# A paged key/value cache loaded as rows of 8 KB, four tokens to a partition, and a bias product that reads its row in that order

## What is computed

```python
PAST_LEN = 4096; PAGE_SIZE = 128; DEC_BATCH = 8; DEC_SEQ = 8; N_HEADS = 8; HEAD_DIM = 64
# cache_k, cache_v (1, 320, 128, 8, 64) float32; page_table (8, 32)
def fox_attend(q, c_q, q_pos, k, v, c_k, k_pos):
    s = jnp.einsum('bqhd,bkhd->bhqk', q, k) * ATTN_SCALE
    bias = jnp.transpose(c_q, (0, 2, 1))[:, :, :, None] - jnp.transpose(c_k, (0, 2, 1))[:, :, None, :]
    s = jnp.where(causal[None, None], s + bias, -jnp.inf)
    p = jax.nn.softmax(s, axis=-1)
    return jnp.einsum('bhqk,bkhd->bqhd', p, v)

def one_seq(args):                       # for each of the 8 sequences
    pages, q_b, k_b, v_b, lf_b = args
    k_all = jnp.concatenate([cache_k[layer, pages].reshape(past, N_KV_HEADS, HEAD_DIM), k_b])
    v_all = jnp.concatenate([cache_v[layer, pages].reshape(past, N_KV_HEADS, HEAD_DIM), v_b])
    c = jnp.cumsum(lf_all, axis=0)
```

## Time and profile before

| | |
|---|---|
| median of 3 runs | 1596.27 us |
| lowest and highest of them | 1588.37 and 1600.27 us |
| span of the profiled execution, first to last instruction | 1590.7 us |
| PE busy | 1400.5 us, 88% of the span |
| DVE busy | 650.0 us |
| ACT busy | 387.5 us |
| mean rate of the DMAs | 267 GB/s |
| mean granted TensorE clock | 0.942 |

### The profile page before, as it was taken

How to read it: one execution, slowest core, us unless ns; L and a number is a source line. 1 busy time by engine, 2 the same in 40 slices (tenths; PEclk the granted TensorE clock), 3 DMA queues, 4 the chain that set the end, 5 groups by cost and what they waited for, 6 DMA issues and landing times. The chain is left out here.

```text
span 1590.7 us, 30783 instructions
## 1 busy us (share of the span) xinstructions
PE 1400.5 (88%) x10030; PEld 745.5 (47%) x10031; DVE 650.0 (41%) x1883; ACT 387.5 (24%) x1026; POOL 249.7 (16%) x291
## 2 busy tenths in 40 slices
PE   6999799999999999699888777777999989999992
PEld 3445566666667776344543322222333333444441
DVE  1423267776586666244543212212222322333333
ACT  1212264444444344311100111111111111111110
POOL 1000200004363220000011111111111111112120
PEclk9999799999999899989899889888999999999996
DMA  8312599999989799660073999999999999975836
GB/s 299 63 27 63 194 308 296 318 304 303 308 266 306 261 319 344 204 237 27 20 291 142 373 374 391 372 372 380 369 368 354 364 371 358 351 235 186 270 82 195
DMA packets 159803, 424.09 MB, mean 267 GB/s; under 512 B 48113, under 2 KB 50194, under 8 KB 133522
## 3 DMA queue, kind: packets, MB, share of 16 engines
q1 hardware_dynamic: 142912, 381.59, 66.5%
q0 software_dynamic: 14688, 38.83, 10.1%
q10 hardware_dynamic: 2098, 2.35, 0.5%
HBM read 395.25 MB, written 42.11 MB: 275 GB/s over the span
## 5 line engine op out<-in xcount | busy, mean ns | idle before, releaser
L2433 PE MATMUL ps_gu<-ring,mixT 128*32 128x512 f32 (+2 forms) x1664 | 368.2, 640 | 69.2 <-SPq L2223 68.3
L2433 PEld LDWEIGHTS ps_gu<-ring,mixT 128*32 128x32 f32 (+2 forms) x1664 | 126.4, 142 | 306.8 <-issue 269.7
L2450 PE MATMUL ps_y<-w_dn,aT_e 128*32 128x512 f32 (+2 forms) x832 | 175.9, 598 | 4.7 <-DVE aT_e L2367 2.5
L1427 PE MATMUL ps_kT<-ident,ring 128*128 128x128 f32 x1024 | 143.2, 282 | 16.5 <-DVE ring L1093 8.9
L1427 PEld LDWEIGHTS ps_kT<-ident,ring 128*128 128x128 f32 x1024 | 115.3, 145 | 74.8 <-issue 45.9
L2365 DVE TENSOR_TENSOR act_in<-sil,ps_gu 128x256 f32<-128x256 f32 x48 | 20.2, 421 | 302.0 <-ACT sil L2305 302.0
L2258 POOL DMA_INDIRECT kT<-h_dram,idx x50 | 51.8, 1037 | 454.5 <-DVE idx L2337 453.9
L2305 ACT ACTIVATE sil<-ps_gu 128x256 f32<-128x256 f32 x48 | 18.4, 383 | 403.9 <-PE ps_gu L2433 403.9
L1093 DVE COPY ring<-ps_kT 128x512 f32<-128x512 f32 x128 | 87.8, 686 | 42.2 <-PE ps_kT L1427 41.2
L2262 POOL DMA_INDIRECT sums_dram<-qT,sidx x50 | 79.9, 1599 | 149.7 <-DVE qT L2372 138.2
L2450 PEld LDWEIGHTS ps_y<-w_dn,aT_e 128*32 128x32 f32 (+2 forms) x832 | 55.4, 132 | 92.5 <-issue 84.2
(11 more groups left out here) (506 smaller groups left out, 1803.0 us busy)
## 6 DMA issues: line engine op xcount, KB each, us to landing
ring<-in_cache_k SPq DMA_DIRECT2D x256, 256.0 KB
ring<-in_cache_v SPq DMA_DIRECT2D x256, 256.0 KB, 4.5
ring<-in_w_gate_e SPq DMA_DIRECT2D x64, 1024.0 KB
ring<-in_w_up_e SPq DMA_DIRECT2D x64, 1024.0 KB
w_dn<-in_w_down_e SPq DMA_DIRECT2D x64, 1024.0 KB
w_in<-in_w_in SPq DMA_DIRECT2D x8, 1028.0 KB, 17.4
sums_dram<-w_dn SPq DMA_DIRECT2D x1, 4608.0 KB, 19.7
ring<-in_w_out SPq DMA_DIRECT2D x1, 4096.0 KB, 13.1
```

The costliest lines, as they stand in the source:

```text
L1427: last = pe.transpose(ps_kT[:, j % 2, e * PAGE:(e + 1) * PAGE], k_places[n % RING][:, e * DA + j * P:e * DA + (j + 1) * P], m.ident[:, :])
L2433: last = pe.matmul(ps_gu[at, :].rearrange("p (g n) -> p g n", g=2), xgT[:, u, k, at], w_gu[:, place, :, k, :].rearrange("p s g n -> p (s g ...
L2450: last = pe.matmul(ps_y[at, n, :], aT[:, j, at], w_dn[:, place, j, n * 512:(n + 1) * 512].rearrange("p s n -> p (s n)"), start=(j == 0), s ...
```

## The change

Each page is loaded into 32 partitions instead of 128: page i of the group goes to partitions i, i+4, i+8 and so on, and each partition takes four tokens that follow each other, one row of 8 KB. So column tile f of a place holds, in partition 4 k + i, token 4 k + f of page i. Keys and values are loaded in the same way, so scores and values agree. The bias row lies in the order of the tokens as before; the product that brings it in now names its 512 columns in the order (f, k, i), whose steps in the bias row are 1, 4 and 128 elements of 2 bytes, with i innermost. The order in which results are written is 0 to 511, as before. No instruction is added, removed or moved on any engine; the DMAs of L740 carry 32 rows of 2048 floats instead of 128 rows of 512.

```diff
@@ pages
             for i in range(GRP):
-                sp.dma_start(place[:, i * DA:(i + 1) * DA], cache[0, bass.ds(ids[i], 1)].rearrange("n k h d -> (n k) (h d)")).then_inc(arrived, 16)
+                sp.dma_start(place[i:P:GRP, :], cache[0, bass.ds(ids[i], 1)].rearrange("n (k f) h d -> (n k) (f h d)", f=FOLD)).then_inc(arrived, 16)
@@ past_scores
-                    pe.matmul(ps_sc[:, :], part_of[:, :, :, :].rearrange("a j e q -> a (j e q)"), bias[:, (n // 2) % 2, (n % 2) * COLS:(n % 2 + 1) * COLS],
-                              start=True, stop=False, skip_group_check=True)
+                    tokens = bias[:, (n // 2) % 2, (n % 2) * COLS:(n % 2 + 1) * COLS].rearrange("a (i k f) -> a f k i", i=GRP, f=FOLD)
+                    pe.matmul(ps_sc[:, :].rearrange("p (f k i) -> p f k i", f=FOLD, i=GRP), part_of[:, :, :, :].rearrange("a j e q -> a (j e q)"),
+                              tokens, start=True, stop=False, skip_group_check=True)
```

## The result

The changed kernel takes 1637.83 us (median of 4 runs, 1629.27 to 1649.23) where the kernel before, run beside it, takes 1598.27 us: a ratio of 1.0256, 95% interval 1.0213 to 1.0298. It is slower by two and a half per cent. The direction of the likeliest case was right; the time is 14 us above the upper end of the range (1590 to 1624 us), and only 0.32 had been given to a kernel slower by more than one per cent. All ratios here compare executions in the usual state of the chip; one of the five executions of e1_again, 6038.76 us, lies outside it and its cause is open. The profiled execution of after has a span of 1632.5 us, 41.8 more than the 1590.7 of before.

What follows compares the result with a forecast made beforehand. The prediction took PE to bound the stage, hiding the page loads. Dearer bias products added 11.1 us (13.4 less 2.3 absorbed), the stores' stall gave back 1.5: + 9.6 us, 1606 us, range 1590 to 1624.

Steps and rivals of the forecast that it cites:

- likeliest case: Whole kernel: 9.6 us slower, about 0.6%, at 1606 us; chance 0.56.
- the loads' gain: Page loads: 0.6 us less DMA time a turn, 38 us over 64 turns, hidden by PE.
- Value taken: 0.21 us, from the rows of the load itself: Bias product: each takes 0.21 us longer, priced from strided against contiguous weight loads; 64 products make 13.4 us.
- upper end: Bias product: 0.52 us longer each, from paces of strided and contiguous transposes; 33 us in all.
- 11 absorbed turns: Turns where PE waits anyway, ten for DVE's copy and one for the store; 2.3 us of added time absorbed there.
- rival 1: Bias product: strided read costs two or more access times a column, 0.52 us each; kernel 26 us slower, 1622 us; chance 0.23.
- both "ends": Bias product's price bounds: 0.01 us each, 1 us in all, and 0.52 us each, 33 us in all.
- part 1: Page loads: larger rows gain 1.5 us at the stores to `y_scr`, nothing elsewhere; bounds nothing and 7.2 us.
- that excess: SP's four page issues ahead of the `y_scr` stores took 0.94 us more than the next four; expected gone.
- the stall: PE stands 5.49 us near 641 us, as ACT waits for SP's stores to `y_scr`; expected about 4 us.
- slack of 4 us: Page loads: pages lie ready at least 4 us before use, so landing up to that much later costs nothing.
- Rival 3: Page loads: writes meet at fewer memory entries, under 286 GB/s; at 250 GB/s 70 us slower, 1665 us; chance 0.05.

Runs made afterwards that it cites:

- e1_again: Second run of the kernel before with only the bias product's reading order changed and the old page loads; ratio 1.0228 (1.0179 to 1.0276).
- experiment 5: Kernel before with its old loads, the bias product reading its row in eight different orders by turns; only each order's product time counted, 385 to 1071 ns.
- experiment 2: Kernel before with only the page loads changed to 8 KB rows on every fourth partition, old reading order; 1598.35 us, ratio 1.0016.
- experiments 7 to 9: Changed kernel's 8 KB rows on 32 neighbouring partitions (two bias reading orders), or every second partition of one half, old order: 1760.35, 1730.42, 1744.37 us.

## Why the prediction was wrong

Right was the frame. PE bounds the stage, it had nothing to do with the loads, the bias product is on PE's path, and its extra time reaches the turn in full but for some waits. The distance to L1443 moved by 0.65 us as the duration did, and the absorbed part was there (5.6 us of 41.1 as measured, about 10 by the table above, of which the rows name 4.7). That the loads' gain "is hidden by PE in all turns and is worth nothing there" held: the loads alone measured 1.0016.

**The step that failed** is the price of one product. The text has "Value taken: 0.21 us, from the rows of the load itself", and an "upper end" of 0.52 us. Measured is 0.652 us. With that value the same sum is 64 x 0.652 = 41.7 us, less 11 absorbed turns (7.2), less 1.5: + 33 us, against the 35.5 and 30.4 that the stage grew by in the two profiles of the changed kernel. That would have been 1629 us, still 9 us under the measured median and at the lower end of its four runs, but on the right side of one per cent. So this term is the miss, but for what the runs scatter by. The sign of being wrong that the prediction had set itself, a product over 0.72 us, came true. That rival 1, which carried 0.52 us, was the nearer case is plain from the row of L1440, though its end was too low as well, and its doubt "the rows with 32 bytes are not slower than those with 8" was drawn from rows of weight loads; for the moving operand 8 bytes took 605 ns and 32 bytes 1071.

Two mistakes of method lie in it. First, the operation priced (a moving operand of 2-byte elements) had no row at all, and a value was borrowed from the way in which TensorE loads weights, 4-byte elements, 128 columns. The borrowed prices did not bound this one; both "ends" came from the same borrowed family and so stood too close. Second, the rule of the Trainium skill that the prediction quotes ("SBUF — State Buffer", section "Door 1: The DMA port swizzle") said where the price must jump, at a new line of 16 bytes, and experiment 5 agrees (394 ns with four elements to a line, 605 with two, 1052 with one). It was set aside because it "gives no price". It could have sorted the rows: in the new order every one of 512 reads opens a new line, in the old one every eighth. The 0.21 us is, by accident, close to the true price of the step of 8 bytes (605 - 385 = 220 ns), in which two reads share a line.

Of part 1, the 1.5 us gained did not come. "With a quarter of the rows I expect that excess gone": it did not go. The longest issues are still 1579 and 1660 ns, and the stall is 4.80 us in one profile and 5.57 in the other, for 5.49. The rate of 368 GB/s of the experts' stage did not come, it stayed at 337. In the records of 300 to 600 us a packet of 2 KB takes 0.084 us in the median and 0.097 in the mean, one of 8 KB 0.309 and 0.386: four small ones take 0.336 and 0.388. The typical row is 8% faster and a tail of long ones (one in ten over 0.63 us) takes it back. What makes that tail is open. "SP's waits for `ps_kT` should grow": they fell from 78.9 to 48 us, because SP itself works longer, 512 x 0.139 = 71 us of issue; the text has no term for that, and the wait for a page in experiment 2 goes with it. One reading of the code needs putting right: `key_pages(n)` waits, by `HP * (n - RING + 1)`, until PE has transposed group n-3, the one in the same place, and not n-2. From there to the use of the new keys it is still two whole turns, so the slack of 4 us stands for the long turns; in the last short ones it was gone.

Rival 3, pages that meet at fewer entries to the memory, did not come true in this kernel, but in experiments 7 to 9: its own limit, 286 GB/s, parts the placement of the change (it would be full at 337) from those on one half (full at 242 to 252). Its working gives 64 x (8.67 - 7.34) = 85 us at 242 GB/s, and the three kernels lost 137 to 167 us against the kernel before beside them. It has no term for PE's clock: in their stages PE spent 133 to 156 us at the lower level, where before had 17. How much of the rest that makes was not taken apart.

## What to carry to other kernels

In such a kernel, count how many successive elements of a moving operand fall into the same 16 bytes before changing its order: with four of 2 bytes it was free, with one a 512-column product took 2.7 times as long. The cheapest place to change an order was where ScalarE or VectorE reads PSUM (no price); writing SBUF in steps cost 1.7 to 4 times the time, and on TensorE the output was cheaper than the input (598 against 1037 ns). Let one DMA reach both halves of the 128 partitions, and expect nothing of larger rows while the engine behind them is the bound; look at the queue that issues them, where a step of partitions made every issue 40% longer. Before two profiles are compared to the microsecond, compare how long each ran at the lower level of the clock.

## What the runs showed of the hardware

- TensorE, moving operand of 2-byte elements, 512 columns: 385 ns with neighbours, 394 with a step of 4 bytes, 605 with 8, 1052 with 16, 1071 with 32, 1015 with 256. With neighbours it is 602 ns at a granted clock of 0.50; in the change's order it is 1.04 us at 0.50 as at 1.00.
- TensorE writing its results to PSUM with neighbours 512 bytes apart: 598 ns for 385.
- ScalarE and VectorE reading 4-byte elements from PSUM with a step of 16 bytes: 585 and 686 ns for 512 columns, as without one; ScalarE with 128 bytes: 694 ns, as without one.
- ScalarE writing 4-byte elements to SBUF with a step of 16 bytes, and VectorE 2-byte elements with one of 64: 2.37 ns an element, against 1.36 (0.694 / 512) and 0.60 (1.23 / 2048). VectorE with one input read from SBUF in steps of 64 bytes: 3.65 us for 2.29.
- DMA into SBUF, 32 rows of 8 KB: 281 GB/s at a share of 83.4% on every fourth partition of the 128 (so 337 when full), full at 242 to 252 on 32 neighbours and at 245 on every second of one half. This fits the map from partitions to ports in the Trainium skill, "SBUF — State Buffer", section "Door 1: The DMA port swizzle".
- SP's issue of such a DMA: 472 ns with a step of four partitions, 467 with a step of two, 316 on neighbours, 333 for 128 rows of 2 KB.
